# Square sums out of the heads of four feed-forward blocks: moved on TensorE, two more groups added by GpSimd, and late T3 and T4

## The reference

```
block 1: h += 0.5 * swiglu(rms_norm(h, g1), 2816 wide)      feed-forward FF0
         h += mix(rms_norm(h)) @ w_out                      attention and RWKV
         h += 0.5 * swiglu(rms_norm(h, g2), 2816 wide)      FF1
         x  = rms_norm(h, final_norm), meta tokens dropped
block 2: new meta tokens, then the same with its own weights: FF2, a gated mixer with w_out_2, FF3
rms_norm(x, g) = x * rsqrt(mean(x * x over the width) + eps) * g
```

## Time and profile before

| | |
|---|---|
| median of 3 runs | 2490.89 us (2489.54 to 2491.67) |
| the profiled execution | 2488.78 us, span 2486.8 us |
| busy: TensorE | 2440.2 us, 98% |
| busy: VectorE | 1705.4 us, 69% |
| busy: ScalarE | 1081.3 us, 43% |
| busy: GpSimd | 98.2 us, 4% |
| mean granted clock of TensorE | 0.984 |

### The profile page before, as it was taken

How to read it: one execution, slowest core, us unless ns; L and a number is a source line. 1 busy time by engine, 2 the same in 40 slices (tenths; PEclk the granted TensorE clock), 3 DMA queues, 4 the chain that set the end, 5 groups by cost and what they waited for, 6 DMA issues and landing times.

```text
span 2486.8 us, 49060 instructions
## 1 busy us (share of the span) xinstructions
PE 2440.2 (98%) x20460; PEld 2245.9 (90%) x20460; DVE 1705.4 (69%) x2926; ACT 1081.3 (43%) x1959; POOL 98.2 (4%) x108
## 2 busy tenths in 40 slices
PE   9999999999999999999999999999989999999998
PEld 7999999996887989898999999898867888989896
DVE  6878675646656879688879684242976445879694
ACT  5444343334434535356535253112874324535352
POOL 0000001000320000001000002000000000000001
PEclk8999999999999999998999999999999999999999
DMA  4233333220001333332233333232212333233322
GB/s 148 85 107 102 102 95 90 81 80 11 4 13 44 103 111 98 107 103 85 73 115 106 99 93 97 71 93 76 55 48 76 92 96 101 100 102 103 102 90 72
DMA packets 72379, 213.01 MB, mean 86 GB/s; under 512 B 12796, under 2 KB 20028, under 8 KB 72032
## 3 DMA queue, kind: packets, MB, share of 16 engines
q1 hardware_dynamic: 70496, 209.03, 26.7%
q0 software_dynamic: 480, 0.73, 0.1%
q10 hardware_dynamic: 1184, 0.12, 0.0%
HBM read 207.61 MB, written 2.20 MB: 84 GB/s over the span
## 4 chain that ended last, share of the span: by engine, by line
PE 87%; DVE 7%; ACT 4%; issue 2%; DVEq 0%; POOL 0%; ACTq 0%; POOLq 0%
PE PS L863 21%; PE PS L1398 20%; PE PS L1355 11%; PE PS L1356 11%; PE PS L1357 11%; DVE WL L948 1%; PE PS L1233 1%; ACT WH L936 1%; PE PS L1706 1%; PE PS L1707 1%; PE PS L1705 1%; PE PS L1319 1%; PE PS L2256 1%; DVE P L2888 1%; PE PS L2825 1%
## 5 line engine op out<-in xcount | busy, mean ns | idle before, releaser
L1355 PE MATMUL PS<-OPH,WH 128*128 128x256 f32 (+1 forms) x2112 | 606.4, 287 | 3.1 <-DVE OPL L1105 2.7
L1357 PE MATMUL PS<-OPH,WL 128*128 128x256 f32 (+1 forms) x2112 | 601.8, 285 | 0.0
L1356 PE MATMUL PS<-OPL,WH 128*128 128x256 f32 (+1 forms) x2112 | 600.2, 284 | 0.0
L936 ACT ACTIVATE WH<-WR 128x1024 fp32r<-128x1024 f32 (+2 forms) x277 | 275.5, 995 | 564.0 <-PE PS L863 272.6
L948 DVE TENSOR_TENSOR WL<-WR,WH 128x1024 fp32r<-128x1024 f32 (+2 forms) x277 | 318.7, 1151 | 191.1 <-ACT WH L936 191.0
L1355 PEld LDWEIGHTS PS<-OPH,WH 128*128 128x128 f32 x2112 | 403.5, 191 | 6.5 <-DVE OPL L1105 3.0
L1356 PEld LDWEIGHTS PS<-OPL,WH 128*128 128x128 f32 x2112 | 403.5, 191 | 2.1 <-issue 1.7
L1357 PEld LDWEIGHTS PS<-OPH,WL 128*128 128x128 f32 x2112 | 402.7, 191 | 0.0
L936 ACT ACTIVATE WH<-SUMS 128x512 fp32r<-128x512 f32 x352 | 211.1, 623 | 229.8 <-DVE SUMS L974 186.6
L948 DVE TENSOR_TENSOR WL<-SUMS,WH 128x512 fp32r<-128x512 f32 x352 | 234.1, 684 | 21.5 <-ACT WH L936 21.2
L863 PE MATMUL PS<-NHI,WH 128*128 128x264 f32 (+2 forms) x960 | 234.5, 309 | 1.5 <-ACT TMP L2623 1.0
(11 more groups left out here) (472 smaller groups left out, 4670.3 us busy)
## 6 DMA issues: line engine op xcount, KB each, us to landing
WR<-in_ffn_up SPq DMA_DIRECT2D x64, 512.0 KB, 3.9
WR<-in_ffn_down SPq DMA_DIRECT2D x64, 512.0 KB, 3.7
WR<-in_ffn_gate SPq DMA_DIRECT2D x56, 512.0 KB, 3.7
WR_MORE<-in_ffn_gate SPq DMA_DIRECT2D x32, 512.0 KB, 4.5
WR_MORE<-in_ffn_up SPq DMA_DIRECT2D x24, 512.0 KB, 4.4
WR<-in_ffn_down SPq DMA_DIRECT2D x32, 384.0 KB, 3.3
WR<-in_w_gate SPq DMA_DIRECT2D x24, 512.0 KB, 3.6
WR<-in_w_out SPq DMA_DIRECT2D x16, 512.0 KB, 3.6
```

The source lines that it names most:

```text
L936: e.activation(split_unit(i)[0][:, 0:w], src, ACT.Copy).then_inc(S["w_hi"], 1)
L1355: e.matmul(o, wh[:, at:at + 128], hi, start=k == 0 and s in (1, 2, 5), stop=False, skip_group_check=True)
L1356: e.matmul(o, wh[:, at:at + 128], lo, start=False, stop=False, skip_group_check=True)
L1357: last = e.matmul(o, wl[:, at:at + 128], hi, start=False, stop=k == 3, skip_group_check=True)
```

## The change

- GpSimd adds the squares of k = 1 to 5 beside both output projections (FF1 and FF3), where it added 1 to 3; TensorE keeps k = 6 and 7. In FF2 GpSimd's part stays k = 1 to 3.
- TensorE's opening sums (the group that GpSimd has added up) move: in FF1 and FF3 to the end of the output projection, with a wait for the add of k = 5; in FF2 to behind ("down", 2, 4), with a wait for all six adds; in FF0 into step (0,1), with k = 1 behind it and k = 4 to 6 into step (0,2), between fillers, of which there are fewer.
- In FF1 to FF3 T3 and T4 of two of the four operands are made behind the split of ab1 instead of between the operands.
- `dve_out` adds to X ahead of the weight splits.

```
-ADDED_BY_POOL = {0: range(0), 1: range(1, 4), 2: range(1, 4), 3: range(1, 4)}
+ADDED_BY_POOL = {0: range(0), 1: range(1, 6), 2: range(1, 4), 3: range(1, 6)}
...
     def act_operands / dve_operands
-            if f and i:
-                act_third(e, q, f, i - 1)
+            if f and i == 1:
+                act_third(e, q, f, 0)
...
-            if f and i:
-                dve_third(e, q, f, i - 1)
+            if f and i == 1:
+                dve_third(e, q, f, 0)
...
-            if f and i > 1:
-                dve_third_low(e, q, f, i - 2)
...
     def act_late_operands
             if f:
-                act_third(e, q, f, 3)
+                for i in range(1, 4):
+                    act_third(e, q, f, i)
...
     def dve_late_operands
             if part == 0 and f:
-                dve_third(e, q, f, 3)
-                dve_third_low(e, q, f, 2)
+                for i in range(1, 4):
+                    dve_third(e, q, f, i)
+                    dve_third_low(e, q, f, i - 1)
...
+        def pe_sums_opened(e, q, f):
+            if f == 2:
+                q.wait_ge("acc", acc_after(3, 3))
+            elif f:
+                q.wait_ge("acc", acc_after(FFN[f][5], ADDED_BY_POOL[f][-1]))
+            else:
+                q.wait_ge("sq", 1)
+            pe_square_sums(e, q, f, None, 0, opens=True)
...
         def pe_sums_after(e, q, f, step):
-            if f == 1 and step in (("down", 2, DT - 2), ("down", 2, DT - 1)):
-                pe_square_sums(e, q, 2, TMP, step[2] - 2, opens=step[2] == DT - 2)
-            if step == ("p", 0, 1):
-                if f == 0:
-                    q.wait_ge("sq", 1)
-                    pe_square_sums(e, q, f, None, 0, opens=True)
-                    for k in range(1, 3):
-                        pe_square_sums(e, q, f, TMP, k)
-                elif f != 2:
-                    q.wait_ge("acc", ACC_BASE[FFN[f][5]] + 3)
-                    pe_square_sums(e, q, f, None, 0, opens=True)
-            if step == ("p", 0, 5):
-                if f == 2:
-                    q.wait_ge("acc", acc_after(4, 3))
-                    q.wait_ge("meta_acc", 1)
-                    pe_square_sums(e, q, f, None, 0)
-                if f == 0:
-                    pe_square_sums(e, q, f, TMP, 3)
-                pe_square_sums(e, q, f, TMP, 6 if f == 2 else 4)
-            if step == ("p", 0, 2):
-                for k in range(7 if f == 2 else 5, DT):
-                    pe_square_sums(e, q, f, TMP, k)
+            if f == 1 and step == ("down", 2, 4):
+                q.wait_ge("acc", acc_after(4, 3))
+                q.wait_ge("meta_acc", 1)
+                pe_square_sums(e, q, 2, None, 0, opens=True)
+            if f == 1 and step[:2] == ("down", 2) and step[2] in (6, 7):
+                pe_square_sums(e, q, 2, TMP, step[2] - 2)
+            if f == 0 and step == ("p", 0, 5):
+                pe_square_sums(e, q, f, TMP, 2)
+                pe_square_sums(e, q, f, TMP, 3)
+            if f > 0 and step == ("p", 0, 5):
+                pe_square_sums(e, q, f, TMP, 6)
+            if step == ("p", 0, 2):
+                pe_square_sums(e, q, f, TMP, 7)
+        def pe_sums_inside(e, q, s, k):
+            if s == 1 and k == 2:
+                pe_sums_opened(e, q, 0)
+                pe_filler(e, q, 1)
+            if s == 1 and k == 3:
+                pe_square_sums(e, q, 0, TMP, 1)
+                pe_filler(e, q, 1)
+            if s == 2 and k > 0:
+                pe_square_sums(e, q, 0, TMP, 3 + k)
+                if k > 1:
+                    pe_filler(e, q, 1)
...
     def pe_step, in the steps (0,1) and (0,2)
-                    if f == 0 and k > (1 if s == 1 else 0):
-                        pe_filler(e, q, 2 if s == 1 else 1)
+                    if f == 0:
+                        pe_sums_inside(e, q, s, k)
...
     def pe_out, behind each product m
+                f = 1 if name == "w_out" else 3
+                if m == 7:
+                    pe_sums_opened(e, q, f)
...
     def dve_out
             for m in range(DT):
+                q.wait_ge("w_used", DONE[name, m])
+                e.tensor_tensor(X[:, m, NM:L], PS[:, out_bank(name, m), 0:SEQ], X[:, m, NM:L],
+                                ALU.add).then_inc(S["w_added"], 1)
                 if name != "w_out":
                     dve_split(e, q, U[name, m] + 2)
                 if name == "w_out" or m == DT - 1:
                     dve_split(e, q, U[name, m] + 3)
-                q.wait_ge("w_used", DONE[name, m])
-                e.tensor_tensor(X[:, m, NM:L], PS[:, out_bank(name, m), 0:SEQ], X[:, m, NM:L],
-                                ALU.add).then_inc(S["w_added"], 1)
                 dve_operands(e, q, f, m)
...
-            pool_squares(e, q, 2, REAL, 4)
+            pool_squares(e, q, 2, REAL, 6)
...
-            pool_squares(e, q, 6, REAL, 4)
+            pool_squares(e, q, 6, REAL, 6)
```

More of the change, by code:

```diff
@@ L742, in wait_all @@
                 q.wait_ge(name, value)
-        ACC_BASE = {1: 0, 2: 7, 5: 16, 6: 23, 7: 26}
+        ACC_BASE = {1: 0, 2: 7, 5: 18, 6: 25, 7: 30}
         def acc_after(s, k):
-            return 10 + 2 * (k - 1) + s - 2 if s in (3, 4) else ACC_BASE[s] + k
+            return 12 + 2 * (k - 1) + s - 2 if s in (3, 4) else ACC_BASE[s] + k
         tmp_of, tmp_end, tmp_next = {}, {x: ("load", 0) for x in range(4)}, [0]
@@ L1222, in pe_square_sums @@
             if opens:
-                q.wait_ge(*free[1])
+                q.wait_ge(*(free[1] if f < 3 else ("w_added", DT + 5)))
             for t in ((4, 3) if f == 2 else (s,)):
@@ L2539, in pe_out @@
                 pe_product(e, q, (name, m), [((name, m), DT)], halves, REAL, "w_used", ready if m == 0 else None)
+                f = 1 if name == "w_out" else 3
+                if m == 7:
+                    pe_sums_opened(e, q, f)
+                for k in range(ADDED_BY_POOL[f][-1] + 1, 6):
+                    if m == 7 if k == 5 else m == 6:
+                        pe_square_sums(e, q, f, TMP, k)
         def act_out(e, q, name, f, s, first):
```

## The result

The changed kernel took 2497.11 us (median of 9 runs) against 2489.74 of the kernel before (9 runs): ratio 1.0030, 95% interval 1.0019 to 1.0042. I had forecast 2489.2 with a range up to 2494.8: the time is 7.9 us above the forecast, and the forecast of "no change" was wrong. Against the kernel before the change is +7.4 us, where I had forecast -1.7.

What follows compares the result with a forecast made beforehand. TensorE, busy 98% of the span, was taken as the bound, so only its waits, other work and clock matter. Terms -2.8 - 5.2 + 3.8 + 2.5 = -1.7 us gave 2490.9 - 1.7 = 2489.2 us, range 2483.0 to 2494.8.

Steps and rivals of the forecast that it cites:

- no change: Whole kernel: time within about 0.2%, 5 us, of the kernel before; chance 0.66.
- GpSimd beside VectorE ... priced at nothing: Output projection w_out: five GpSimd adds block VectorE about 1.0 us in all, hidden by spare time; 0, bounds 0 to 6.3.
- the surplus of 2.7: VectorE's rounds beside w_out: 8.8 us saved by the earlier X add, less 6.1 needed, leaves 2.7 us to spare.
- GpSimd's lock eats the lead: Rival, w_out: five adds at 1.26 us lengthen rounds by 6.3, X(7) 3.6 late; sum +1.9, 2492.8 us; chance 0.08.
- FF1, -5.2 forecast: Head of FF1: X(7) 6.1 us earlier, TensorE waits 3.2 us for r1; gain 6.8 or 4.3, taken as 5.2.
- The late T3 and T4 cost: FF1 to FF3: T3 and T4 behind ab1's split make T4H 1.85 us later, counted from X(7); 2.1 in FF2.
- the slower row: Steps (0,6), (1,1), (1,2): 7.12 us with part of the matmuls at the lower clock, against 4.27 at full clock.
- FF2, +3.8 forecast: Behind down step 4: 3.2 us wait for GpSimd, 1.9 of sums, then lower clock; 3.8 us lost, bounds 0.6 and 5.7.
- FF3, +2.5 forecast: Head of FF3: T4H 2.3 us later, (0,7) already waiting for r2; 2.3 lost, 3.3 at lower clock, taken as 2.5.
- FF0, -2.8 forecast: Head of FF0: TensorE reaches (0,6) early, waits for r1, (0,7) starts at 44.3; 2.8 us gained, bounds 1.4 and 3.0.
- near 31.4 at full clock: FF0: TensorE reaches step (0,6) near 31.4 instead of 40.56; anything before 37.3 gives the same.
- slower by over 0.2%: Whole kernel over 5 us slower: needs two slow rivals at once (lock with clock, +6.1) or a missed price; chance 0.12.

Runs made afterwards that it cites:

- the second measurement of the same kernel: The changed kernel, nothing altered, measured once more against the kernel before: ratio 1.0025 (1.0015 to 1.0035).
- the fastest version: Kernel before with one edit, the X add ahead of the weight split in w_out alone: 2484.58 us, 0.9978; again 2484.06 us, 0.9976.

## Why the prediction was wrong, step by step

- **"GpSimd beside VectorE ... priced at nothing" is the step that failed.** I reasoned that an add starts when VectorE does the X add, which reads PSUM, so that only 0.2 of its 1.4 us would block. It started 2.55 us behind the start of the X add (784.77 to 787.32, timeline above), since the square comes late in ScalarE's round, just ahead of T1, and held T1 for 1.03 us. The trace of before had the hint: there it started 2.23 behind the X add (782.57 to 784.80), not with it. With two adds more the lock took more than the surplus of 2.7: 5 x 1.03 = 5.2 us in the rounds. The rival "GpSimd's lock eats the lead", which I gave 0.08, named place and mechanism; its price for the five was 6.3, its lag of X(7) 3.6, and 2.35 was measured. Without the two adds X(7) lay 0.2 behind the product, as forecast. The Trainium skill, "SBUF — State Buffer", section "Who interferes with whom", said that an instruction of VectorE with two SBUF inputs and one of GpSimd that reads SBUF exclude each other for the whole instruction; the trace agrees, five times out of five. The X add, which takes one input from PSUM, met no add beside w_out; in FF2 an operation with one input in PSUM (L1546, at 1136.21) lay inside an add and took its 0.68 us, as elsewhere. I had set that rule aside on an assumed place of the add in the round. In the ledger FF1 is 3.3 of the 7.4 us between forecast and sum, 2.15 of them this lag; GpSimd back to k = 1 to 3, with its sums in TensorE's wait, gave 5 to 6 us.
- **FF1, -5.2 forecast, -1.9 measured.** The late T3 and T4 cost was right (T4H 8.4 behind X(7), 1.86 more than before); X(7) was 2.15 too late, TensorE's wait for r1 5.15 instead of 3.2, and the steps behind it took 6.87, near the slower row (7.12), where I took a value between. With the slower row I had -4.3; -4.3 + 2.15 = -2.2.
- **FF2, +3.8 forecast (0.6 to 5.7), +5.2 measured.** Mechanism and place were right: a wait of 3.03, 18 sums, a lower clock. The size was too small by 1.4, within the bounds. By one profile 3.5 of it are the pause's own, and 1.7 come only when T3 and T4 are late as well.
- **FF3, +2.5 forecast (2.3 to 3.3), +3.0 measured.** T4H came 3.0 later (2138.63, 10.4 behind w_out_2) and not 2.3: 1.85 by T3 and T4 (10.4 - 0.6 - 1.85 - 0.6 = 7.4), 0.6 by the X add ahead (I had 0.5), and 0.6 because X(7) started 0.77 behind the product instead of 0.20. That last part isn't the adds alone: in the second measurement of the same kernel all five adds hold VectorE too, and X(7) starts at 0.20 and T4H at 9.8. There VectorE waited 0.40 us for the DMA of a gate weight ahead of X(5), here 2.17. (0,7) waited for TensorE and not for r2 in this profile, since the steps behind the wait for r1 were granted 0.63.
- **FF0, -2.8 forecast (-1.4 to -3.0), -2.0 in the ledger.** The count "near 31.4 at full clock" did not hold: TensorE came to (0,6) at 37.9 to 43.5, at half clock, because the small sums let the clock fall. I had used full clock for a stretch, 27 to 38 us, that was granted 0.62 in before. And the unedited stretch behind it is 1.4 us longer, which eats most of it: undone in pairs it gives 0.3 us, added to before it costs 0.7, on the fastest version it gives 1.7. I can't tell it from nothing.
- **The chances.** I gave "slower by over 0.2%" 0.12, holding that two slow rivals would have to come together. The lock did come, and FF2 and FF3 were each a little over; the terms that I had taken from the middle of their bounds all erred to one side. No single rival gives +7.4: the lock as I had priced it, with the rest as forecast, is +1.9.

What stays open: whether the 1.4 us in unedited code follow from FF0 or are chance (the profiles scatter by 6 us there), why FF2's length behind the pause varies from 361.9 to 365.0 (the last with the waits filled), and why the three steps of a head without a wait have full clock in some profiles and not in others.

## What to carry to other kernels

Before giving GpSimd work "for free", lay its instruction on the timeline of the round and list the VectorE operations with two SBUF inputs that can start inside it: each add costs the one it meets what is left of it (here 1.03 to 1.11 of 1.3 to 1.6 us), and a VectorE that is the lagging engine pays in full. When sums or copies are moved off a critical engine, check when their input is ready at the new place; one step later was free here, one step too early cost 6 us. Undo each part of a bundle: of this one a single edit (the X add ahead, in w_out) was worth 5.5 to 6 us, and the rest took it back and more.

## What was unexpected of the hardware

- A wait of TensorE is paid again behind it: after waits of 4 to 5 us for r1 three steps of 4.3 us took 6.5 and 6.9 (granted 0.63 and 0.59), and with matmuls without a use in the wait 4.35 and 4.66 at 1.00. But a wait isn't needed for it: without one the same steps were granted 0.56 to 0.75 in 14 of 23 heads.
- Matmuls of one column keep TensorE "busy" in the profile, but in FF0, where they stand between products and fillers, the clock fell to 0.50; with six groups of ten replaced by four wide ones each it was 1.00. A block of 18 of them behind products didn't lower it at once (1.00 in the earlier trace rows and in FF2's opening sums one step later).
- The same unchanged instructions ran at 1.00 in one execution and at 0.55 in the other. Stage lengths of one profile pair are good to 2 or 3 us in this kernel; my first reading of FF0 (+3.2) was such a draw.
